# Delta masks, latent tiles and the shared key's rotation: an order of work changed in a two-block fp32 kernel

## The reference, cut to what matters

```python
# gated delta rule, chunk of 64, 4 heads of 128
gc = jnp.cumsum(g_of_chunk, axis=-1)
decay = jnp.exp(jnp.where(tril, gc[..., :, None] - gc[..., None, :], -jnp.inf))
a_mat = jnp.where(strict, einsum('bnhid,bnhjd->bnhij', kbeta, kc) * decay, 0.0) + jnp.eye(C)
sol = lax.linalg.triangular_solve(a_mat, rhs, left_side=True, lower=True, unit_diagonal=True)
attn = jnp.where(tril, einsum('bnhid,bnhjd->bnhij', qc, kc) * decay, 0.0)
def step(state, inp):
    v_new = u_n - einsum('bhck,bhkv->bhcv', w_n, state)
    o = einsum('bhck,bhkv->bhcv', q_n * jnp.exp(g_n)[..., None], state) + einsum(..., a_n, v_new)
    ...
# latent attention, 8 heads
qm = (rmsnorm(mq, mla_q_norm) @ mla_w_uq)      # mq: 384 wide, three tiles of 128
kv = (rmsnorm(mkv, mla_kv_norm) @ mla_w_ukv)   # mkv: 256 wide, two tiles
q_pe = apply_rope(qm[..., MLA_NOPE:], cos, sin)
k_pe = apply_rope(mkr[:, :, None, :], cos, sin)  # one key of 64, shared by the heads
def apply_rope(t, cos, sin):
    rot = jnp.concatenate([-t[..., half:], t[..., :half]], axis=-1)
    return t * cos + rot * sin
```

## Time and profile before

| | us |
|---|---|
| median of 3 runs | 2174.23 |
| lowest and highest of them | 2172.2, 2174.31 |
| profiled execution | 2169.36 |
| its span | 2167.6 |
| PE busy | 2066.5 (95%) |
| DVE, ACT, POOL busy | 1244.5, 883.6, 604.3 |

### The profile page before, as it was taken

The page is one execution under the profiler, slowest core; times in us unless marked ns, Lnnn a source line. Parts: engine busy times, 40 slices in busy tenths (PEclk is TensorE's granted clock), DMA queues, the critical chain, the costliest instruction groups (busy, mean ns, idle before and its releaser), DMA issues. The chain is left out here.

```text
span 2167.6 us, 28014 instructions
## 1 busy us (share of the span) xinstructions
PE 2066.5 (95%) x10952; PEld 1533.1 (71%) x10952; DVE 1244.5 (57%) x1984; ACT 883.6 (41%) x1412; POOL 604.3 (28%) x280
## 2 busy tenths in 40 slices
PE   8999999999999999999999899999999988989997
PEld 6667874757768775667786766677877766767776
DVE  4688945547679855456658733535145875254342
ACT  4432355333432345333455333445234733144531
POOL 2323430233314421124343200123433431002252
PEclk9999999998999999998999999999999999999998
DMA  6223321232223231132322012113232210111232
GB/s 222 85 96 107 112 78 49 68 136 98 99 81 117 78 102 59 53 122 83 117 88 68 22 40 78 49 49 102 98 117 78 88 50 22 59 49 39 63 114 86
DMA packets 47857, 180.02 MB, mean 83 GB/s; under 512 B 5646, under 2 KB 6286, under 8 KB 46320
## 3 DMA queue, kind: packets, MB, share of 16 engines
q1 hardware_dynamic: 47600, 178.11, 24.3%
q10 hardware_dynamic: 128, 0.13, 0.0%
HBM read 163.54 MB, written 14.68 MB: 82 GB/s over the span
## 5 line engine op out<-in xcount | busy, mean ns | idle before, releaser
L2431 POOL TENSOR_TENSOR w_lo<-wraw,w_hi 128x1024 fp32r<-128x1024 f32 x220 | 547.3, 2489 | 1412.6 <-ACT w_hi L1188 1412.6
L1188 ACT ACTIVATE w_hi<-wraw 128x1024 fp32r<-128x1024 f32 x220 | 232.8, 1058 | 666.1 <-PE bank L611 413.8
L597 PE MATMUL bank<-h_hi,w_hi 128*128 128x512 f32 x1568 | 409.0, 403 | 1.1 <-ACT h_hi L1212 1.1
L606 PE MATMUL bank<-h_lo,w_hi 128*128 128x512 f32 x1568 | 390.5, 391 | 0.2
L611 PE MATMUL bank<-h_hi,w_lo 128*128 128x512 f32 x1536 | 379.6, 389 | 0.0
L597 PEld LDWEIGHTS bank<-h_hi,w_hi 128*128 128x128 f32 x1568 | 292.6, 190 | 92.3 <-issue 32.6
L606 PEld LDWEIGHTS bank<-h_lo,w_hi 128*128 128x128 f32 x1568 | 295.9, 189 | 64.6 <-DVE h_lo L1728 1.7
L611 PEld LDWEIGHTS bank<-h_hi,w_lo 128*128 128x128 f32 x1536 | 288.4, 188 | 59.8
L714 PE MATMUL bank<-arena,wdir 128*128 128x512 f32 x256 | 114.7, 599 | 1.2 <-DMA wdir<-in_w_direct 1.2
L868 PE MATMUL bank<-arena,wdir 128*128 128x512 f32 x208 | 100.2, 613 | 0.0
L2337 DVE TENSOR_TENSOR bank<-bank,con 128x128 f32<-128x128 f32 x64 | 19.2, 300 | 134.0 <-PE bank L1104 133.1
(11 more groups left out here) (384 smaller groups left out, 3121.3 us busy)
## 6 DMA issues: line engine op xcount, KB each, us to landing
wraw<-in_w_split SPq DMA_DIRECT2D x220, 512.0 KB, 3.3
wdir<-in_w_direct SPq DMA_DIRECT2D x44, 512.0 KB, 3.3
x_park<-arena SPq DMA_DIRECT2D x3, 2048.0 KB, 6.2
arena<-x_park SPq DMA_DIRECT2D x3, 2048.0 KB, 8.0
hg_park<-arena SPq DMA_DIRECT2D x2, 2048.0 KB, 8.6
arena<-hg_park SPq DMA_DIRECT2D x2, 2048.0 KB, 8.2
arena<-bias_rows SPq DMA_DIRECT2D x2, 1792.0 KB, 7.4
arena<-in_xT SPq DMA_DIRECT2D x2, 1024.0 KB, 7.2
```

What stands on the lines that cost most here:

```text
L597: mm(ps[0:wd, 0:S], hi[:, k, :].bitcast(F32R), h_hi[:, k, :].bitcast(F32R), start=k == 0 and not begun, stop=False)
L606: ins = mm(ps[0:wd, 0:S], hi[:, k, :].bitcast(F32R), h_lo[:, k, :].bitcast(F32R), start=False, stop=bool(parts) and k == KT - 1)
L1188: a(w_hi[:, n % 2, 0:f].bitcast(F32R), wraw[:, n % 2, 0:f], ACT.Copy).then_inc(hi_done, 1)
L2431: nc.gpsimd.tensor_tensor(w_lo[:, n % 2, 0:f].bitcast(F32R), wraw[:, n % 2, 0:f], w_hi[:, n % 2, 0:f], ALU.subtract).then_inc(lo_done, 1)
```

## The change

There are three moves of code; no instruction is added or left out.

```diff
# ACT
                 keep(("mq", l, 0), cq[:, 0, :])
+                keep(("mq", l, 1), cq[:, 1, :])
                 for tt in range(NT):
                     act.wait_ge(*after("dclip", l, tt))
                     a(dtm[:, tt, :, :], dtm[:, tt, :, :], ACT.Exp).then_inc(up("dexp", l, tt), 1)
-                keep(("mq", l, 1), cq[:, 1, :])
                 keep(("mq", l, 2), cq[:, 2, :])
...
-                swap_halves(kr, tmp[:, 0, :], "kr_rot", l)
                 for j in range(5):
...
                 for n in range(1, len(LEVELS)):
...
+                    if n == 2:
+                        swap_halves(kr, tmp[:, 0, :], "kr_rot", l)
                     if n >= 3:
                         turn_queries(n - 3)
# DVE
                     dve.wait_ge(*read("gB", l, h, 0))
+                for h in range(H):
                     dve.wait_ge(*after("egb", l, h))
                     link(v.tensor_copy(egl[:, h, :], qg[:, h, CH - 1:S:CH]))
                     v.tensor_tensor(qg[:, h, :], qg[:, h, :], qB[:, h, :], ALU.mult)...
-                dve.wait_ge(*after("kr_rot", l))
-                link(v.tensor_tensor(kr[:, :], kr[:, :], cosT, ALU.mult))
-                link(v.tensor_tensor(tmp[:, 0, :], tmp[:, 0, :], sinT, ALU.mult))
-                v.tensor_tensor(kr[:, :], kr[:, :], tmp[:, 0, :], ALU.add).then_inc(up("kr", l), 1)
...
+                    if n == 2:
+                        rotate_keys()      # the four lines above
                     if n == 3:
```

More of the change, by code:

```diff
@@ L2193, in _ @@
                     dve.wait_ge(*after("qg", l, h))
-                dve.wait_ge(*after("kr_rot", l))
-                link(v.tensor_tensor(kr[:, :], kr[:, :], cosT, ALU.mult))
-                link(v.tensor_tensor(tmp[:, 0, :], tmp[:, 0, :], sinT, ALU.mult))
-                v.tensor_tensor(kr[:, :], kr[:, :], tmp[:, 0, :], ALU.add).then_inc(up("kr", l), 1)
-                dve.wait_ge(*after("kr", l))
                 def gcols(tt, r):
@@ L2241, in _, with rotate_keys @@
                 dve.wait_ge(*read("qk", l, NT - 1))
+                def rotate_keys():
+                    dve.wait_ge(*after("kr_rot", l))
+                    link(v.tensor_tensor(kr[:, :], kr[:, :], cosT, ALU.mult))
+                    link(v.tensor_tensor(tmp[:, 0, :], tmp[:, 0, :], sinT, ALU.mult))
+                    v.tensor_tensor(kr[:, :], kr[:, :], tmp[:, 0, :], ALU.add).then_inc(up("kr", l), 1)
+                    dve.wait_ge(*after("kr", l))
                 def rotate(h):
```

## The result

| | before | changed |
|---|---|---|
| median us | 2173.22 (4 runs, 2171.74 to 2174.31) | 2156.5 (4 runs, 2155.79 to 2158.7) |
| profiled execution, its span | 2169.36, 2167.6 | 2155.79, 2154.0 |
| ratio, 95% interval | | 0.9925 [0.9908, 0.9942] |

The account below looks back on a forecast made before the run. PE, busy 95% of the span, was taken as the bound, so only its waits and half clock could be won. Terms 0.8 + 3.2 = 4.0 us per layer, twice 8.0, took 2174.23 to 2166.2 us; range 2160.0 to 2170.4.

Parts of the forecast that it names:

- The clip held until POOL is done: Delta masks: DVE's clip, held beside POOL's remainder until 1172.7, ends some 1.15 us later; `mq` 2 gains 1.05 us.
- the first `kk` tile held and harmless: Delta products: POOL's remainder holds DVE's first `kk` tile until about 1198.7, yet DVE stays 1.5 to 2 us ahead.
- the cover of 4.83 us at the border: Border of n = 2 and n = 3: DVE's 4.83 us wait for PE covers the moved rotation, costing nothing, at most 0.5.
- given back at the border: Rival, chance 0.20: half clock reaches the rotary queries at n = 2 to n = 3, costing 2.2 us per layer; 2170.6.
- nothing arrives: Rival, chance 0.05: another engine or a transfer ends last further down; median within 1 or 2 us, 2173.
- slower: Rival, chance 0.03: the clock stays at 1.2 GHz past `mq` 2, both `mkv` tiles run at half clock; 2186.
- Part 3: Delta products: rotation moved away; column sums 2.8 us earlier, `vN` 3.2 us earlier per layer, bounds 2.8 to 3.2.
- the wait of `P`: Last `P` product of n = 1 waits 0.4 us for DVE's `Mt`; this wait goes too.
- Part 1: Delta masks: `mq` 1's bank emptied ahead of the exponentials; 0.8 us per layer, bounds 0.55 and 4.6.
- the wait ahead of the column sums: Delta products: PE ends chunk products at 1198.67, starts column sums at 1201.80; the shared key holds PE.
- a little over 1 us per layer of luck with the clock: Lower bound of the main forecast: the clock going the other way gives 2164.0 us.
- more: Rival, chance 0.17: the clip is not held, or the clock returns sooner or does not fall; middle 2161.

Follow-up runs that it names:

- the first comparison: First measurement of the changed kernel against the kernel before: median 2156.5 us against 2173.22, ratio 0.9925.
- again_before: The kernel before the change, unchanged, measured and profiled a second time: median 2172.67 us, ratio 1.0001.
- third_before: The kernel before the change, unchanged, as one more entry: median 2173.55 us, ratio 1.0005.
- repeat_rows: Changed kernel with norm rows 5 to 7 made three times and the eighth nine times, filling PE's wait ahead of `mq` 2: 2163.92 us.
- pool_and_full: Changed kernel with POOL's remainder waiting for the clip and full-height matmuls added ahead of all eight norm rows: 2168.99 us.
- full_rows: Changed kernel with full-height matmuls added ahead of the fifth to eighth norm row, filling the wait ahead of `mq` 2: 2163.62 us.

## Why the prediction was right or wrong

**Which step failed.** The places and the order of events were right. Two things in the sum were not. The wait that the change removes was mis-sized: 4.0 us per layer where the intervals show 4.97. And the clock outside `mq` 2 was put at nothing: over 19 and 100 executions the medians differ by 13.5 us, 3.6 more than the waits, and between the profiled executions a difference of that size is half clock. The rest of the 16.7, 3.2 us, is what the first comparison had by chance.

**Right: what bounds the three places, and the order of events.** The clip held until POOL is done (forecast 1.15 us late, measured 1.12), `mq` 2 1.05 us earlier (1.12), the first `kk` tile held and harmless, the squares straight behind the last `mkv` tile, the cover of 4.83 us at the border. The rival *given back at the border* did not come: in all four executions of the changed kernel the first `qr` tile starts within 0.15 us of the usual time after `kN`. Nor did *nothing arrives* or *slower*: both `mkv` tiles ran at full clock in all.

**Part 3, a term too small.** "PE ends the chunk products at 1198.67 and needs some 0.35 us to go on" was the wrong step. The products and the column sums follow each other with no gap once nothing is waited for, and the term is 3.20 instead of 2.8. And the wait of `P` was 0.65 us, not 0.4: I took it as the excess of 2.60 over the 2.15 of `X0`, but `P` without the wait takes 2.03 and starts 0.09 sooner behind `X0`. Together 3.85 per layer, beyond the stated bound of 3.2. "PE then has no wait left from 1199.0 on" had the same 0.35 in it.

**Part 1, a discount that was not needed.** I took 0.8 of the 1.05 us for fear that the clock's return stays where it is. The wait was 1.12 shorter. From `mq` 2 to the gate rows the changed kernel took 7.44 to 8.48 us, the kernel before 6.99 to 8.27, so over executions some of it may be lost after all; both are within the spread.

Together these are 4.97 instead of 4.0 per layer, 9.94 instead of 8.0. That accounts for 2 us of the miss.

**The base.** The sum was read from one profiled execution and taken off a median of three. That median, 2174.23, is 2.0 us above the median of 100 executions. With the right waits, the same step would have given 2164.3. Below that lie the 5.6 us to 2158.7: 2.0 of them are the base, the other 3.6 the half clock that the changed kernel has less, in the stretch of the change (1.5) and elsewhere. Whether the part elsewhere comes with the change stays open.

**The hidden cost of a wait.** The prediction read the wait ahead of the column sums from an execution in which it was followed by full clock (windows at 1.00), and so priced it at its length. In three of the four places of `again_before` and `third_before` the clock fell in it or 1.2 us behind it. The prediction had this mechanism for `mq` 2, where the trace showed it, and never asked it of the other wait of 3.13 us. It even worked out a clock that moves between executions, but only as a loss (*given back*).

**The range.** It allowed "a little over 1 us per layer of luck with the clock", where executions of one kernel spread over 6 us, and its lower end came from single terms of part 1. The case named *more* is nearest to the result (2161 against a lasting median of 2158.7) but for another reason than the one given: the clip was held, and the clock at `mq` 2 did fall.

## What to carry to other kernels

Price a wait of PE at its length and then ask whether the clock can fall in it: look at the granted clock in every such wait and just behind it, and in more than one execution if they are to be had. Compare kernels by intervals between fixed instructions; here those without a fall of the clock repeat within 0.04 us while totals move by 5. And take away what makes PE wait rather than fill the wait with added matmuls: the removal gave 9.94 us that every trace shows, while filling gave 1 or 2 us at one place and lost 3 to 10 at the other.

## What the runs showed of the hardware

- PE with matmuls of four rows is busy without a gap in the windows from 1171 to 1174 of `repeat_rows`, and its granted clock falls to 1.2 GHz at 1171.3. With full-height matmuls between such rows it stayed at 2.4 GHz in one layer of `pool_and_full` and one of `full_rows`, and fell in the other of each.
- The moments at which the clock changes move between executions of one program, as the Trainium skill says (TensorE: Matmul & The Clock Gate, Part 1, there of the moment at which it rises). Here the whole amount of half clock was 106.9, 120.6, 110.2 and 110.3 us in four executions of the changed kernel, and executions of the kernel before spread from 2168.89 to 2174.94 us.
- DVE beside POOL: a clip of four 128x256 tiles with a constant takes 2.02 us instead of 0.90 beside the end of a 128x1024 remainder, and a product of two SBUF tensors 2.49 instead of 0.42. Beside POOL's short 128x256 instructions the two engines share the loss: DVE's products of 128x512 took 0.77, 1.10 and 1.10 us instead of 0.69, and POOL's three instructions 3.00 instead of 2.11.
